# High halves of the weights 96 bytes past a 128-byte boundary instead of 64, and output projections whose matmuls take high and low columns woven in runs of 16

## What is computed

```python
# first layer
h = rms_norm(x, mix_norm);  z = h @ w_in                  # 256x2048 @ 2048x12040
merged = sigmoid(g_a)*(y_a @ wb_a) + sigmoid(g_b)*(y_b @ wb_b) + sigmoid(g_c)*(y_c @ wb_c)
x = x + merged @ w_out                                    # 2048x2048, output projection
x = x + conv_ffn(rms_norm(x, ffn_norm), w_up, conv_w, conv_b, w_down)   # 2048x11264, 5632x2048
x = rms_norm(x, final_norm)
# second layer
proj = rms_norm_2(x, g_mix) @ w_in_2
x = x + (g[0]*y_a + g[1]*y_b) @ w_o_2                     # 2048x2048, output projection
x = x + (silu(gt) * up) @ w_down_2                        # after w_gate_up_2, 2048x11264
```

## Time and profile before

| | |
|---|---|
| time, median of 3 runs | 2975.9 us (2974.11 to 2978.74) |
| profiled execution, span from the first to the last instruction | 2978.0 us |
| PE busy | 2946.2 us, 99% of the span |
| PE weight loads busy | 2630.0 us, 88% |
| DVE busy | 2051.0 us, 69% |
| ACT busy | 1311.7 us, 44% |
| mean granted TensorE clock | 0.998 of full speed |

### The profile page before, as it was taken

One profiled execution on the slowest core, in us unless ns is written; L12 is line 12 of the kernel. 1 busy time (PEld: TensorE's weight loads), 2 busy tenths in 40 slices (PEclk: granted clock), 3 DMA queues, 4 the chain that ended last, 5 costly groups with the idle time before them and its releaser, 6 DMA issues.

```text
span 2978.0 us, 47097 instructions
## 1 busy us (share of the span) xinstructions
PE 2946.2 (99%) x18616; PEld 2630.0 (88%) x18616; DVE 2051.0 (69%) x2624; ACT 1311.7 (44%) x1418; POOL 70.0 (2%) x72
## 2 busy tenths in 40 slices
PE   8999999999999999999999999999999999999999
PEld 8898898999988888888888888876998888888888
DVE  6675787977788888885557776636666666666444
ACT  5354423444444444444444354425445444444333
POOL 0000000000001000000000000000000000000000
PEclk9999999999999999999999999999999999999999
DMA  6553334555555555555555544531555555555555
GB/s 230 184 183 134 114 120 149 168 173 198 186 196 193 189 196 194 190 182 190 193 195 198 195 172 168 186 122 43 184 198 186 195 197 188 193 197 177 194 193 184
DMA packets 87359, 530.39 MB, mean 178 GB/s; under 512 B 9952, under 2 KB 10336, under 8 KB 41184
## 3 DMA queue, kind: packets, MB, share of 16 engines
q1 hardware_dynamic: 87264, 529.07, 50.7%
HBM read 526.94 MB, written 2.10 MB: 178 GB/s over the span
## 4 chain that ended last, share of the span: by engine, by line
PE 96%; DVE 2%; ACT 1%; DMA 0%; issue 0%; SPq 0%; DVEq 0%; ACTq 0%
PE bank L576 74%; PE late L576 22%; DVE arena L1687 1%; DVE w_low L1687 0%; DVE half_low L1687 0%; DVE arena L1684 0%; ACT w_high L1203 0%; PE late L1144 0%; DVE arena L1989 0%; DMA ring<-in_w_gates 0%; DMA xT<-in_xT 0%; DVE acts_both L1687 0%; DVE arena L2045 0%; DVE arena L2016 0%; DVE xrs L1734 0%
## 5 line engine op out<-in xcount | busy, mean ns | idle before, releaser
L1687 DVE TENSOR_TENSOR w_low<-ring,w_high 128x2048 fp32r<-128x2048 f32 (+1 forms) x480 | 1014.3, 2113 | 384.1 <-ACT w_high L1203 380.2
L1203 ACT ACTIVATE w_high<-ring 128x2048 fp32r<-128x2048 f32 (+1 forms) x480 | 849.5, 1771 | 636.0 <-DMA ring<-in_w_down 223.0
L576 PE MATMUL bank<-up_early,w_high 128*128 128x512 f32 x1408 | 487.8, 389 | 0.0
L576 PE MATMUL bank<-up_late,w_high 128*128 128x512 f32 x1408 | 487.3, 389 | 0.0
L576 PE MATMUL late<-acts_both,w_high 128*128 128x512 f32 x1408 | 479.0, 389 | 0.3 <-DVE w_low L1687 0.3
L576 PE MATMUL bank<-up_early,w_low 128*128 128x256 f32 x1408 | 388.6, 276 | 0.0
L576 PE MATMUL late<-acts_both,w_low 128*128 128x256 f32 x1408 | 388.6, 276 | 0.0
L576 PE MATMUL bank<-up_late,w_low 128*128 128x256 f32 x1408 | 388.6, 276 | 0.0
L576 PEld LDWEIGHTS bank<-up_early,w_high 128*128 128x128 f32 x1408 | 264.5, 188 | 55.2
L576 PEld LDWEIGHTS late<-acts_both,w_high 128*128 128x128 f32 x1408 | 264.3, 188 | 55.1 <-DVE w_low L1687 0.6
L576 PEld LDWEIGHTS bank<-up_late,w_high 128*128 128x128 f32 x1408 | 264.0, 188 | 54.7
(11 more groups left out here) (311 smaller groups left out, 4946.2 us busy)
## 6 DMA issues: line engine op xcount, KB each, us to landing
ring<-in_w_up SPq DMA_DIRECT2D x176, 1024.0 KB, 4.7
ring<-in_w_down SPq DMA_DIRECT2D x128, 704.0 KB, 4.0
ring<-in_w_in SPq DMA_DIRECT2D x66, 1024.0 KB, 4.7
ring<-in_w_mix SPq DMA_DIRECT2D x62, 1024.0 KB, 4.8
ring<-in_w_gates SPq DMA_DIRECT2D x96, 512.0 KB, 3.7
ring<-in_w_branch SPq DMA_DIRECT2D x16, 1024.0 KB, 4.7
ring<-in_w_out SPq DMA_DIRECT2D x16, 1024.0 KB, 4.8
ring<-in_w_o SPq DMA_DIRECT2D x16, 1024.0 KB, 4.8
```

The costliest lines, as they stand in the source:

```text
L576: return nc.tensor.matmul(o, lhsT, rhs, start=first, stop=last)
L1203: A(w_high[:, s, 0:cols], ring[:, s, 0:cols], ACT.Copy).then_inc(rounded[s], 1)
L1687: return V.tensor_tensor(o, a, b, op)
```

## The change

It does two things.

1. `W_SHIFT` goes from 960 to 992. `w_high` then stands 96 bytes past a 128-byte boundary, for ACT and DVE, which write and read it, and for each matmul that loads it.
2. In both output projections `project_pairs` is replaced by `project_woven`. The moving operand of the matmul of 512 columns is the same two tiles, but read as 16 columns of the high tile, 16 of the low one, the next 16 of the high one, and so on. A row of the PSUM bank so holds high and low results in turn, in runs of 16. The matmul of 256 columns still reads the high tile in one piece, but adds into each second run of 16 of the bank. DVE's two adds per unit read each second run of 16 in place of one half of the bank.

```diff
-W_SHIFT = 960
+W_SHIFT = 992
+BLOCK = 16
...
+            def project_woven(both, waits=None):
+
+                def body(s):
+                    o = bank_row[s].rearrange("p (n a b) -> p n a b", a=2, b=BLOCK)
+                    for k in range(KT):
+                        if waits:
+                            waits(k)
+                        c = slice(k * P, (k + 1) * P)
+                        x = both[:, :, k].rearrange("p a (n b) -> p n a b", b=BLOCK)
+                        mm(o, w_high[:, s, c], x, k == 0, False)
+                        last = mm(o[:, :, 0], w_low[:, s, c], x[:, :, 0], False, k == KT - 1)
+                    return last
+                return body
...
-                pairs = [both[:, :, k] for k in range(KT)]
-                unit_split(project_pairs(pairs, waits))
+                unit_split(project_woven(both, waits))
                 for j in range(3):
-                    unit_split(project_pairs(pairs))
-                rounds_split(3, project_pairs(pairs))
+                    unit_split(project_woven(both))
+                rounds_split(3, project_woven(both))
...
-                    link(tt(xT[:, n], xT[:, n], bank[s][:, 0], ADD))
-                    tt(xT[:, n], xT[:, n], bank[s][:, 1], ADD).then_inc(drained[s], 1)
+                    two = bank_row[s].rearrange("p (n a b) -> p n a b", a=2, b=BLOCK)
+                    x = xT[:, n].rearrange("p (n b) -> p n b", b=BLOCK)
+                    link(tt(x, x, two[:, :, 0], ADD))
+                    tt(x, x, two[:, :, 1], ADD).then_inc(drained[s], 1)
```

## The result

The changed kernel takes 3018.75 us (median of 4 runs, 3017.4 to 3021.65) against 2977.32 us for the kernel before, measured beside it. The ratio of the two kernels is put at 1.0142, with a 95% interval of 1.0124 to 1.016; the two medians divided give 1.0139. (Ratios here are estimates from all runs of both kernels, so they can differ a little from the quotient of the medians.) The prediction said 2969 us and a range up to 3004 us. The change is slower, and by more than the range held.

What follows compares the result with a forecast made beforehand. PE's rhythm was taken to bound the kernel. The terms 0 - 5.6 - 1.5 + 0 = -7.1 us, from a median of 2975.9 us, gave 2968.8, stated as 2969 us; range 2945 to 3004 us.

Steps and rivals of the forecast that it cites:

- What bounds the kernel: Whole kernel: PE, busy 99%, sets the time; 20 ns beyond streaming on each of 5664 pairs, 113 us at stake.
- Part 1: Loads of w_high moved from 64 to 96 bytes, in 5152 pairs and 1056 triples: 0 taken as likeliest single value.
- halving by distance: Moved w_high loads: 96 bytes is 32 from 64 and 32 from the next boundary, so +3.5 ns, +18 us.
- the shift costs: Matmuls of 256 columns beside moved w_high loads get slower: 2987 us, or 3021 us in the 350 ns rhythm; chance 0.28.
- far end: All 5152 pairs with moved w_high lock into the 350 ns rhythm: +52 - 7, 3021 us; a third of the 0.28.
- The bounds of part 1: Moved w_high loads: pairs -31 to +36 us, triples -23 to +7 us; the other rhythm in all pairs +52 us.
- Part 2: Woven matmul of 512 columns in the output projections: 216 ns, the fp32 row, -11 ns x 512 = -5.6 us.
- The upper bound: Woven matmul of 512 columns: if each of 31 jumps cost a cycle, 13 ns, +7 us.
- Part 3: Matmul of 256 columns in the output projections, writing PSUM in runs: -3 ns x 512 = -1.5 us; bounds -3, +53 us.
- Part 4: DVE's adds reading PSUM in runs, and ACT and DVE using w_high at another offset, stay within slack: 0.

Runs made afterwards that it cites:

- the shift alone: The kernel before with W_SHIFT 992, so w_high at 96 bytes past a boundary in place of 64, no weave: 3010.07 us, ratio 1.0093.
- the weave alone: The changed kernel with w_high back at 64 bytes, woven output projections kept: 2993.03 us, ratio 1.0030 against the kernel before.

## Why the prediction was wrong

- **What bounds the kernel** was right: PE's rhythm, in ns a pair, times 5664 pairs. No other engine came into it; in the output projection DVE waited longer for PE than before ahead of its adds (1.62 us in place of 1.01), the adds took 0.88 us.
- **Part 1 failed, and decided the result.** The step was "I take 0 for this part", chosen because rhythms sit at a few fixed values. Rhythms do sit at a few values, but that was no reason for 96 to share the value of 64. Measured: +6.7 ns in the up projections, +30 us in all between the spans of the shift alone and before. The halving by distance, +3.5 ns, was nearer and still half of it. The rival "the shift costs" came true; it was given 0.28. Its far end, 3021 us, is near the measured 3018.75 by luck: it had all pairs at 350 ns and a weave that gains 7 us, where most pairs stood at 346.7 and the weave costs 7 to 10 us. And its mechanism, that the matmul of 256 columns beside the moved load pays, was half of it: in the up projections the matmul of 512 columns got longer by as much, 3.3 ns. The trace of before could have told more: the same pair at 350 ns in the earlier trace rows was treated as an oddity of few pairs, while it was evidence that the loop at 64 bytes already stood in the better of two rhythms, with something to lose.
- **The bounds of part 1 were made from the wrong rows.** The gates' 120 ns gave a ceiling of 347 a pair at offset 0; measured 352. A pair isn't the sum of what its two loads cost elsewhere. The range was too narrow even by these bounds: +36 us for pairs and +7 for triples on top of 2969 are 3012 us, and it ended at 3004.
- **Part 2 had the wrong sign.** The woven matmul was taken at -11 ns, from full-fp32 matmuls that ask for columns at half pace. Measured with the weave alone: +13 ns in its mean duration (402 against 389) and +20 ns for the pair. The upper bound, +7 us for jumps, was short too: +10 us.
- **Part 3**: PSUM in runs costs nothing, where the Trainium skill, "SBUF — State Buffer", Door 1, expects non-contiguous PSUM access to slow matmuls significantly; in runs of 16 fp32 values the measurement is 389 and 276 ns with and without. The 256 columns behind a woven stream got 5 to 10 ns longer, where 3 less were forecast.
- **Part 4** was right: adds from PSUM in runs stay within DVE's slack.
- **What I left out**: the parts aren't additive, stage by stage. The piece with the output projection got 1.20 us longer by the shift, 5.11 by the weave and 4.65, not 6.31, by both. The first down projection takes 241.24 us with both and 235.20 with the shift alone, at the same addresses. The ratios can't tell this: 1.0093 and 1.0030 make 1.0123, against 1.0142 for both, with intervals of 0.001 to 0.002 to each side.
- The Trainium skill's sentence in "TensorE: Matmul & The Clock Gate", Part 2, that loading the next weights takes nothing from the running matmul, isn't borne out: in kernels that differ only in where the buffers of loaded weights stand, the same two matmuls take 340 to 353 ns. Whether it is read bandwidth that is lost, no run shows.

Which unit inside PE or SBUF holds the streams up stays open, and so does what exactly picks a rhythm at an entry. The runs show only that the rhythms that occur differ with the offsets, and that a few matmuls ahead of a stage can change which one it gets. No version beat the kernel before. Of the eight pairs of offsets measured, its own (w_low at 0, w_high at 64) is the only one at which any long stage had 340 ns; but each of the others was measured with one way into each stage, and a better rhythm behind another entry isn't excluded.

## What to carry to other kernels

Where weights are loaded beside every matmul, measure the distance between starts, per block and per stage, before and after: a few ns on thousands of pairs are per cents, and here they changed with steps of 32 bytes in the place of a buffer. (That the pattern repeats every 128 bytes is assumed; no run moved a buffer by 128 bytes alone.) Change one offset at a time with everything else as it is, and look at every stage that shares the buffer, not at the one that the change is for. An unrelated matmul ahead of a long loop can cost more than it contains, so a stage that got slower without an edit of its own isn't proof of a dependency; compare its rhythm first.

## What the runs showed of the hardware

- The same loop at the same addresses has several steady rhythms and keeps the one it falls into for over a thousand pairs: 340 and 350 ns with w_low at 0 and w_high at 64; 344.9, 346.7 and 353.7 with w_high at 96; 348.9 and 353.3 with both at 64; 347.0 and 353.3 with w_low at 64 and w_high at 0. These are means over pieces of the chain. The granted clock was 0.997 of full speed or more in all of these profiles.
- Offsets in bytes past a 128-byte boundary, and the first up projection's pair: w_low 0 with w_high 0, 32, 64, 96: 352.0, 349.4, 340.0, 346.7 ns. w_high 64 with w_low 0, 32, 64, 96: 340.0, 349.3, 353.3, 348.9 ns. w_low 64 with w_high 0: 353.3.
- Matmul output in runs of 16 fp32 columns in PSUM costs PE nothing (389 and 276 ns, as before). A moving operand read in turn from two tiles costs 20 ns a pair in runs of 16 columns and 13 in runs of 32, with w_low at 0 and w_high at 64; with both at 64, runs of 16 cost 5 in the first layer and 9 in the second.
- Three fp32 matmuls ahead of both up projections made the kernel 38 us longer in 2980, 1.3 us of it by their own work and the rest by the rhythm of the stages behind them; one made no difference that shows.
